# Two more seven-product pairs in a hybrid attention and RG-LRU layer, with the branch tiles of block 0 and the gates of block 1 interleaved

## What is computed

```python
proj = einsum('bsd,de->bse', x, w_in) + b_in
q, k, v, g_attn, x_rnn, g_rnn, m_attn, m_rnn = split(proj)
attn = window_attention(rope(q), rope(k), v, sink) * silu(g_attn)
xc = depthwise_conv4(x_rnn, conv_w, conv_b)              # 10 blocks of 128 channels
r = sigmoid(xc @ wa + ba); i = sigmoid(xc @ wx + bx)     # per direction and block
a = exp(-8 * r * softplus(-lam)); u = sqrt(1 - a * a) * (i * xc)
rnn = (scan_forward(a, u) + scan_backward(a, u)) * silu(g_rnn)
merged = sigmoid(m_attn) * (attn @ w_branch_attn) + sigmoid(m_rnn) * (rnn @ w_branch_rnn)
x = layernorm(alpha * x + merged @ w_out + b_out)
```

## Time and profile before

| | us |
|---|---|
| median of 3 runs | 1028.35 (1028.26 to 1028.65) |
| profiled execution | 1029.07 |
| its span | 1027.3 |
| PE busy | 1009.8 |
| DVE busy | 670.9 |
| POOL busy | 618.0 |
| ACT busy | 471.8 |

### The profile page before, as it was taken

One profiled execution on the slowest core, in us unless ns is written; L12 is line 12 of the kernel. 1 busy time (PEld: TensorE's weight loads), 2 busy tenths in 40 slices (PEclk: granted clock), 3 DMA queues, 4 the chain that ended last, 5 costly groups with the idle time before them and its releaser, 6 DMA issues.

```text
span 1027.3 us, 12975 instructions
## 1 busy us (share of the span) xinstructions
PE 1009.8 (98%) x4641; PEld 836.1 (81%) x4641; DVE 670.9 (65%) x769; ACT 471.8 (46%) x687; POOL 618.0 (60%) x378
## 2 busy tenths in 40 slices
PE   8999999999999999999999999999999999999997
PEld 6888888888888888878887888787887878888885
DVE  4946665503556653666587886877878488839756
ACT  4054445221554465573758466574856741102021
POOL 5654435446543422535499999999999734485223
PEclk9999999999999999999999999999999999999999
DMA  8264333565524121435262534435243788937012
GB/s 330 98 240 134 126 120 113 178 239 187 168 78 163 53 71 52 143 106 192 65 218 76 154 102 136 130 115 164 84 142 84 242 296 322 341 99 295 1 47 118
DMA packets 65861, 154.69 MB, mean 151 GB/s; under 512 B 6928, under 2 KB 7312, under 8 KB 65680
## 3 DMA queue, kind: packets, MB, share of 16 engines
q1 hardware_dynamic: 56880, 131.36, 38.7%
q10 hardware_dynamic: 8928, 22.64, 5.7%
HBM read 108.88 MB, written 45.09 MB: 150 GB/s over the span
## 4 chain that ended last, share of the span: by engine, by line
PE 83%; POOL 7%; DVE 4%; issue 3%; DMA 2%; ACT 1%; SPq 0%; DVEq 0%; POOLq 0%; ACTq 0%
PE proj L863 13%; PE proj L865 13%; PE proj L864 13%; PE proj L1067 6%; PE proj L1071 5%; PE proj L1073 5%; POOL w_lo L751 5%; PE aux L863 3%; PE aux L865 3%; PE aux L864 3%; PE aux L927 3%; PE aux L909 2%; POOL w_hi L764 2%; PE proj L1184 1%; PE proj L1183 1%
## 5 line engine op out<-in xcount | busy, mean ns | idle before, releaser
L716 POOL TENSOR_SCALAR w_hi<-raw 128x1024 fp32r<-128x1024 f32 (+1 forms) x46 | 62.5, 1358 | 246.1 <-PE proj L863 190.4
L863 PE MATMUL proj<-xt_hi,w_hi 128*128 128x512 f32 x476 | 192.2, 404 | 0.2
L865 PE MATMUL proj<-xt_hi,w_lo 128*128 128x512 f32 x476 | 186.4, 392 | 0.0
L864 PE MATMUL proj<-xt_lo,w_hi 128*128 128x512 f32 x476 | 186.2, 391 | 0.0
L751 POOL TENSOR_TENSOR w_lo<-raw,w_hi 128x512 fp32r<-128x512 f32 x66 | 123.7, 1879 | 4.4
L719 POOL TENSOR_TENSOR w_lo<-raw,w_hi 128x1024 fp32r<-128x1024 f32 (+1 forms) x46 | 123.4, 2682 | 3.8
L865 PEld LDWEIGHTS proj<-xt_hi,w_lo 128*128 128x128 f32 x476 | 89.3, 188 | 19.7
L863 PEld LDWEIGHTS proj<-xt_hi,w_hi 128*128 128x128 f32 x476 | 89.6, 188 | 15.7 <-DVE xt_lo L1604 0.8
L864 PEld LDWEIGHTS proj<-xt_lo,w_hi 128*128 128x128 f32 x476 | 89.6, 188 | 14.1
L1067 PE MATMUL proj<-xt_hi,w_hi 128*128 128x512 f32 x224 | 87.8, 392 | 1.5 <-POOL w_lo L751 1.5
L1073 PE MATMUL proj<-xt_hi,w_lo 128*128 128x512 f32 x224 | 87.2, 389 | 0.0
(11 more groups left out here) (199 smaller groups left out, 2467.6 us busy)
## 6 DMA issues: line engine op xcount, KB each, us to landing
raw<-stream SPq DMA_DIRECT2D x52, 512.0 KB, 4.2
presum_a<-stream SPq DMA_DIRECT2D x42, 256.0 KB, 2.9
sums<-presum_a SPq DMA_DIRECT2D x42, 256.0 KB, 2.0
raw<-sums SPq DMA_DIRECT2D x38, 256.0 KB, 2.8
spill<-part ACTq DMA_DIRECT2D x16, 512.0 KB, 3.1
merges<-stage_out ACTq DMA_DIRECT2D x32, 256.0 KB, 3.6
raw<-stream SPq DMA_DIRECT2D x31, 256.0 KB, 2.7
raw_half<-stream SPq DMA_DIRECT2D x21, 256.0 KB, 2.8
```

Of the source, the lines that this page charges most:

```text
L716: nc.gpsimd.tensor_scalar(hi, raw[:, raw_slot, cols], 1.0, 0.0, ALU.mult, ALU.add)\
L863: begun = nc.tensor.matmul(bank, wh, mov_hi, start=first, stop=False)
L864: nc.tensor.matmul(bank, wh, mov_lo, start=False, stop=False)
L865: return begun, nc.tensor.matmul(bank, wl, mov_hi, start=False, stop=last)
```

## The change

`PLAIN` becomes 1 and the list of pairs loses its first merge pair and starts at block 1: pair 0 is (x3, g1), pair 1 (x4, g2), pair 2 merge 0, and so on, 16 pairs. The plain tiles x3, x4, g1 and g2 go. The four branch tiles of block 0 and the first of block 1 stand together behind gates(0, 1), the other three between and behind the gates of block 1. Four more weight presums are spread over the units by a list. T1 is split by POOL behind product 1 of pair 0, T4 and T2 stay with ACT and DVE, and the loads of T1 and T2 move behind the first four half loads. On DVE block 1's scans stand behind block 2's convolution and T3's low part.

```diff
-PLAIN = 3
-TWINS = [(("merge", 0, 0), ("merge", 0, 1))]
+PLAIN = 1
+TWINS = []
 for _b in range(PLAIN, RNN_BLOCKS):
     if _b < RNN_BLOCKS - 1:
         TWINS.append((("x", _b + 2) if _b < RNN_BLOCKS - 2 else ("g", _b + 1), ("g", _b)))
-    TWINS.append((("merge", _b - 2, 0), ("merge", _b - 2, 1)))
+    if _b > PLAIN:
+        TWINS.append((("merge", _b - 2, 0), ("merge", _b - 2, 1)))
...
+_hosts = [u for u in range(FIRST_PRESUM, UNIT_B) for _ in range(2 if u in (4, 6, 8, 10, 12, 19, 21, 23, 24, 25) else 1)]
...
@@ SP
-            for name in NAMES_B[:10]:
+            for name in NAMES_B[:6]:
                 load_unit(name)
-            for step in range(6):
+            for step in range(2):
                 load_t(step)
...
                     if i == 3 and q == 0:
+                        for step in range(2, 6):
+                            load_t(step)
+                    if i == (2 if q else 5) and q not in MERGES:
+                        load_gates(TWINS[q][1][1] + 1)
+                    if i == 5 and q == 0:
                         load_t3(0)
                         load_t3(1)
-                        load_gates(PLAIN)
...
-            sp.wait_ge(product_split, PRODUCTS - 4)
+            sp.wait_ge(product_split, PRODUCTS - 2)
             load_branch(0)
@@ POOL
+            def t1_part(c):
+                hi, lo, _, plain = t_home[1][0]
+                ks = slice(2 * c, 2 * c + 2)
+                pool.wait_ge(t_landed[2 + c], 16)
+                nc.gpsimd.tensor_scalar(hi[:, ks, :], plain[:, ks, :], 1.0, 0.0, ALU.mult, ALU.add)\
+                    .then_inc(t1_hi_done, 1)
+                pool.wait_ge(t1_hi_done, c + 1)
+                nc.gpsimd.tensor_tensor(lo[:, ks, :], plain[:, ks, :], hi[:, ks, :].bitcast(f32), ALU.subtract)\
+                    .then_inc(t1_split, 1)
             def twin_weights(q, gates_of):
                 for i in range(7):
                     split_half(7 * q + i)
-                    if i == 3 and gates_of:
+                    if q == 0 and i == 1:
+                        for c in range(2):
+                            t1_part(c)
+                    if i == (3 if q else 4) and gates_of:
                         gate_weights_half(gates_of)
@@ PE
+            gates(0, 0)
+            branch(0, 0)
+            gates(0, 1)
+            for t in range(1, 5):
+                branch(t // 4, t % 4)
+            gates(1, 0)
+            branch(1, 1)
+            gates(1, 1)
+            branch(1, 2)
+            branch(1, 3)
+            rnn_tile(("x", 2), 0)
+            for i in range(7):
+                twin_product(0, i)
+            for b in range(PLAIN + 1, RNN_BLOCKS):
+                first = merge_of(b) if twin_of(b) is None else twin_of(b)
+                early = 4 if b == PLAIN + 1 else 1
+                gates(b, 0)
+                for i in range(early):
+                    twin_product(first, i)
                 gates(b, 1)
+                for i in range(early, 7):
+                    twin_product(first, i)
                 if twin_of(b) is not None:
+                    for i in range(7):
                         twin_product(merge_of(b), i)
@@ ACT, blocks 1 and 2
+            act.wait_ge(rnn_done, 1)
+            sigmoids(1, 0)
...
+            t_high(4)
+            t_high(5)
+            pad_x(2, FILLS["x", 2])
+            conv_begin(2, FILLS["x", 2])
+            early_copy(0, 0)
+            t3_high(0)
+            t3_high(1)
+            early_copy(0, 1)
+            conv_high(2)
+            early_copy(0, 2)
+            early_copy(0, 3)
+            sigmoid_of(1)
@@ DVE, block 1
+            scan_input(1)
+            t_low(4)
+            t_low(5)
+            for tap in range(1, CONV_W):
+                conv_tap(2, tap)
+            t3_low(0)
+            t3_low(1)
+            conv_low(2)
+            scans(1)
+            for number in range(4):
+                twin_sum(0, number)
+            state_sum(1)
+            silu_of(1)
+            gated_state(1)
```

More of the change, by code:

```diff
@@ L139 @@
 PRESUMS = [[] for _ in range(UNIT_B)]
-_parts = [(q, part) for q in range(len(TWINS)) for part in range(2)]
-for _n, _part in enumerate(_parts):
-    PRESUMS[FIRST_PRESUM + _n * (UNIT_B - FIRST_PRESUM) // len(_parts)].append(_part)
+_hosts = [u for u in range(FIRST_PRESUM, UNIT_B) for _ in range(2 if u in (4, 6, 8, 10, 12, 19, 21, 23, 24, 25) else 1)]
+for _n, _part in zip(_hosts, [(q, part) for q in range(len(TWINS)) for part in range(2)]):
+    PRESUMS[_n].append(_part)
 def branch_bank(b, t):
-    return t % 2 if b == 0 else 1 - t % 2
+    return t % 2
 FILLS_GROUP = HEADS + 1 + 4
@@ L163, in fills_b @@
     place(("x", 1), 0)
-    for b in range(PLAIN):
-        if b < 2:
-            for t in range(4):
-                place(("branch", b, t), branch_bank(b, t))
-        if b:
-            place(("g", b), 1)
-        place(("x", b + 2), 0)
+    for t in range(8):
+        place(("branch", t // 4, t % 4), branch_bank(t // 4, t % 4))
+    place(("x", PLAIN + 1), 0)
     return found, tuple(count)
@@ L834, in _ @@
                     twin_weights(twin_of(b), b + 1)
-                twin_weights(merge_of(b), None)
+                if merge_of(b) is not None:
+                    twin_weights(merge_of(b), None)
             for name in NAMES_D:
@@ L1474, in _, with spill_tile @@
                             spill_branch(g, 2 * n + b, b, g * FILLS_GROUP + HEADS + 2 + n)
-            def spill_tile(b, t):
-                if b < 2:
-                    spill_branch(N_GROUPS - 1, 4 * b + t, branch_bank(b, t), FILLS["branch", b, t])
+            def spill_tile(t):
+                b = t // 4
+                spill_branch(N_GROUPS - 1, t, branch_bank(b, t % 4), FILLS["branch", b, t % 4])
             silu_gate(0)
             act.wait_ge(attn_split, 2 * N_HEADS + 2)
-            for b in range(RNN_BLOCKS):
+            pad_x(1, FILLS["x", 1])
@@ new lines, in _ @@
+            sigmoids(0, 0)
+            conv_begin(1, FILLS["x", 1])
+            spill_tile(0)
+            sigmoids(0, 1)
+            decay_tanh(0)
+            conv_high(1)
+            decay_exp(0)
+            decay_square(0, 0)
+            spill_tile(1)
+            decay_square(0, 1)
+            roots(0)
+            for t in range(2, 5):
+                spill_tile(t)
+            t_high(0)
+            t_high(1)
+            act.wait_ge(rnn_done, 1)
+            sigmoids(1, 0)
+            store_state(0)
@@ new lines, in _ @@
+            spill_tile(5)
+            sigmoids(1, 1)
+            decay_tanh(1)
+            decay_exp(1)
+            spill_tile(6)
+            decay_square(1, 0)
+            spill_tile(7)
+            decay_square(1, 1)
+            roots(1)
+            t_high(4)
[7 more added lines that the diff above has]
+            conv_high(2)
@@ L1484, in _ @@
+            early_copy(0, 2)
+            early_copy(0, 3)
+            sigmoid_of(1)
+            for b in range(PLAIN + 1, RNN_BLOCKS):
                 last_one = b == RNN_BLOCKS - 1
                 q, m = twin_of(b), merge_of(b)
-                if b > PLAIN:
-                    early_copy(m - (2 if q is not None else 1), 3)
-                if b < PLAIN:
-                    pad_x(b + 1, FILLS["x", b + 1])
-                if b:
-                    act.wait_ge(rnn_done, b)
-                sigmoids(b, 0)
@@ L1497, in _ @@
+                if merge_before is not None:
+                    merge_gate(merge_before, 2)
+                    merge_gate(merge_before, 3)
+                if q is not None and b > PLAIN + 1:
                     early_copy(q, 0)
@@ L1508, in _ @@
                 decay_tanh(b)
-                if b == 2:
-                    t_high(3)
                 if not last_one:
@@ L1913, in _ @@
             dve.wait_ge(attn_split, 2 * N_HEADS + 2)
-            for b in range(RNN_BLOCKS):
+            gated_input(0)
+            for tap in range(1, CONV_W):
+                conv_tap(1, tap)
+            conv_low(1)
+            one_less_decay(0, 0)
+            one_less_decay(0, 1)
+            scan_input(0)
+            scans(0)
+            gated_sum(0)
+            t_low(0)
+            t_low(1)
+            gated_input(1)
+            one_less_decay(1, 0)
+            one_less_decay(1, 1)
+            scan_input(1)
+            t_low(4)
+            t_low(5)
+            for tap in range(1, CONV_W):
+                conv_tap(2, tap)
[8 more added lines that the diff above has]
+            gated_state(1)
+            for b in range(PLAIN + 1, RNN_BLOCKS):
                 last_one = b == RNN_BLOCKS - 1
                 q, m = twin_of(b), merge_of(b)
-                if b >= PLAIN:
-                    twin_sum(m - (2 if q is not None else 1), 2)
-                    twin_sum(m - (2 if q is not None else 1), 3)
+                if merge_of(b - 1) is not None:
+                    twin_sum(merge_of(b - 1), 2)
+                    twin_sum(merge_of(b - 1), 3)
                 gated_input(b)
```

175 lines of the change are left out of this document (53 added, 122 removed).

## The result

The changed kernel takes 1041.38 us (median of 4 runs, 1040.81 to 1041.80) against 1028.50 for the kernel before beside it (4 runs, 1028.26 to 1028.98): a ratio of 1.0124, interval 1.0107 to 1.0142, so 12.9 us slower. The profiled execution took 1040.81 with a span of 1039.0. I had forecast 1033.5, slower, with 1037 as the upper end: the direction is right, the size is 8 us short and outside the range.

The account below looks back on a forecast made before the run. PE was taken as the bound, POOL within a few per cent of one. Terms: -5.44 (matmuls) - 2.06 (waits gone) + 7.26 (behind gates(2,1)) + 5.35 (W0) = +5.1 us, giving 1033.5, range 1025.5 to 1037.

Parts of the forecast that it names:

- W0: PE's waits in pair 0, on POOL's late weight splits: 5.35 us, moving everything behind them.
- the presums at nothing: Four extra presum parts, 8 short POOL operations in the attention stage, costed at no time; without cover 8 x 1.3 us.
- the wait behind gates(2,1): Pair 1: product 4 waits for POOL, which first splits block 3's gate weights; 7.26 us, range 4.9 to 7.5.
- The bound and the matmuls: Whole kernel: PE bounds it, POOL nearly; 24 matmuls less at 0.2268 us each save 5.44 us of PE.
- T0: Start of gates(0,0), 394.80 in the kernel before; the working counts PE's matmuls from there.
- DVE has no pause then: Pair 0: second sum, taps, third sum, low part and scans follow one another, so POOL's mean pace was taken.
- The rival with the scans: Pair 0: scans slow POOL's products 5 and 6 to 5.8 + 3.8 us; W0 8.5, time 1036.6, chance 0.18.
- The low end by POOL's pace: Behind gates(2,1): gate split and product split at POOL's quick pace, with starts some 4.2 us.
- ACT's floor: Pair 1: product 6 needs ACT's early copy, 10.4 us after the gates against 5.44 of products; wait at least about 4.9.
- Edits at nothing: Extra presums, spills, ACT's t_high work and moved loads, priced at no time; first branch unit's load up to 1 us.
- The point of decision: The change decides for faster once W0 plus the wait behind gates(2,1) is below 7 us.
- The first rival: POOL at quick pace in pair 0: W0 0, gate split 4.9 instead of 7.26; change -2.8, 1025.5, chance 0.2.

Follow-up runs that it names:

- the last experiment: Another list of double presum units, in the changed kernel with T1 off POOL, high parts on ACT and pair 1 reordered: 1028.12 us, ratio 0.9987.
- POOL's order mended: Changed kernel with POOL's gate split of block 3 behind product 6 of pair 1 instead of product 3: 1040.96 us, ratio 1.0115.
- kernel with W0 of 0.5 and the wait of 5.4: Changed kernel with T1 split by ACT and DVE, and `w_hi` of products 3 to 6 of pair 0 made by ACT: 1031.50 us, ratio 1.0024.

## Why the forecast was right in sign and short in size

The step that failed is the sum for W0: it priced POOL's splits in pair 0 with the mean of a stage (W0 5.35, measured 12.33) and had no term for half clock behind a wait. The second is the presums at nothing (some 1.8 us). Both pushed the time up, and 2.9 us of them were hidden by an error the other way, the wait behind gates(2,1).

**The bound and the matmuls: right.** 4617 matmuls, pitch 0.2268, the x2 tile at T0 + 54.43, blocks 4 to 8 at 44.2 to 44.3.

**W0: the right mechanism, the wrong size**, 12.33 for 5.35. I had priced a saturated stretch with the mean of a stage that has quiet moments in it. Term by term, with the start corrected for the 2.39 us of the attention stage: T1 began when I had said (456.95 - 2.39 = 454.56, forecast 454.5) but took 10.7, not 8.4 (+2.3); the agreement of the start is luck, since I had it wait for its load with POOL free at 453.7, while in the trace POOL was still at product 1's `w_lo` (2.14 us for 1.29); products 2 to 4 took 3.76 each, not 3.25 (+1.5); the gate split took 5.76, not 2.65 (+3.1); product 5 took 1.96, not 3.25 (-1.3). That puts product 5 5.6 us later than forecast, of which 0.5 was slack against product 6. The other 1.6 us are slow matmuls, for which the sum had no term at all. 5.1 + 1.6 make 6.7 of the 6.98.

**"DVE has no pause then": the right observation, and I took the wrong row for it.** It should have led me to the rows of 1.59 beside taps and 2.60 beside scans, which stood in the earlier trace rows, and not to the mean of the earlier trace rows. The rival with the scans had that in it, but laid them over products 5 and 6 (W0 of 8.5); they fell on the gate split, and the slow products came ahead of them. By 1036.6 it was the nearest case that I gave. I had named the rule behind it, of the Trainium skill (SBUF — State Buffer, Who interferes with whom), that such DVE and GpSimd operations exclude each other. The runs agree: with DVE's operations cut to 8 columns, the same gate split took 0.62 and 1.29 us. The same section of the Trainium skill says that whoever issues first keeps the other out; the 118.30 presum against `q_lo` (2.31 for 1.22) agrees, and this direction I had not thought of.

**The wait behind gates(2,1): there, by far the longest after pair 0, but 4.37 and not 7.26.** POOL did wait for gates(2,1) (11.36 us idle at 510.54) and PE for product 4, as forecast. But the taps had ended at 510.44 (506.51 + 3.93) just before, so POOL ran at its quick pace, 0.62, 1.26, 0.62, 1.27. The low end by POOL's pace, 4.2, was the value; I had raised it to 4.9 by ACT's floor. In before's block 3 the same work lay beside the taps; I had carried this overlap over without asking where the taps would be after W0.

**Edits at nothing: wrong for the presums, right for the rest.** I had asked what POOL has to spare in the attention stage, and not what DVE would lose. That is some 1.8 of the 2.39 us, the rest being a later start; the last experiment took it away with nothing but another list. Of the moved loads, the spills and ACT's t_high no trace shows a wait of PE.

**The floor of ACT: there, but lower.** It can't be seen in after. With POOL's order mended it stood at product 6, as named, but 519.63 - 510.77 (end of the gates) = 8.9 us behind the gates and not 10.4, so that the wait was 3.42 and not 4.9. The row that I took it from is of a block where DVE's taps took 5.36 us, not 3.93.

**The point of decision: short of two terms.** I had put it at 7 us for W0 and the wait behind the gates together; my own sum gives 7.5 for a time below before's, and 5.4 for one below 1026.3. (The first rival has a like slip: 7.26 less 4.9 is 2.36, not 2.6.) The two waits were 16.7, so the verdict held. In the kernel with W0 of 0.5 and the wait of 5.4 they were 5.9, and it still was 0.24% slower, because of 2.2 us of half clock and 1.8 in the attention stage that the sum didn't have.

## What to carry to other kernels

When an edit gives work to POOL, lay it beside DVE's timeline, operation by operation, and price it with the rows that stand beside the same kind of DVE operation, and price what it does to DVE too; the mean of a stage is no price for a stretch where DVE never pauses. An in-order engine that waits for a shared buffer in the middle of its list needs its consumer to have work meanwhile: four products put ahead of gates instead of one moved their cover away. And a long wait of PE costs more than its length, so several short ones are cheaper than one of the same sum.
